# The bias of the last layer norm of block 2 moves from ScalarE to GpSimd, and ScalarE squares the tile before the bias is added

## The reference, cut to what matters

```python
def _layer_norm(x, g, b):
    mu = jnp.mean(xf, -1, keepdims=True)
    var = jnp.mean(jnp.square(xf - mu), -1, keepdims=True)
    return ((xf - mu) * lax.rsqrt(var + LN_EPS) * g + b).astype(x.dtype)

h = _layer_norm(ALPHA * h + ff + ple, ln2_g[i], ln2_b[i])     # end of block 2

def _rmsnorm(x, w):
    y = xf * lax.rsqrt(jnp.mean(xf * xf, axis=-1, keepdims=True) + NORM_EPS)
    return (y * w).astype(x.dtype)

h = _rmsnorm(x, norm_w[l])                                    # start of block 3
proj = h @ w_in[l] + b_in[l]
```

## Time and profile before

| | |
|---|---|
| median of three runs | 3994.99 us |
| the profiled execution's own time | 3996.76 us |
| its span, first to last instruction | 3995.0 us |
| mean granted TensorE clock | 0.983 of full |
| PE busy | 3836.1 us, 96% |
| DVE busy | 1816.0 us, 45% |
| ACT busy | 796.1 us, 20% |
| POOL busy | 592.4 us, 15% |

### The profile page before, as it was taken

The page is one execution under the profiler, slowest core; times in us unless marked ns, Lnnn a source line. Parts: engine busy times, 40 slices in busy tenths (PEclk is TensorE's granted clock), DMA queues, the critical chain, the costliest instruction groups (busy, mean ns, idle before and its releaser), DMA issues.

```text
span 3995.0 us, 32255 instructions
## 1 busy us (share of the span) xinstructions
PE 3836.1 (96%) x12831; PEld 1955.9 (49%) x12831; DVE 1816.0 (45%) x2613; ACT 796.1 (20%) x977; POOL 592.4 (15%) x630
## 2 busy tenths in 40 slices
PE   8999999999899899989999999999899999899998
PEld 4555444544346776454444444444356554544554
DVE  8576434435655542255633232324645553424432
ACT  2112111111452211351310000000323320221121
POOL 0343210122112220132122222222000000000000
PEclk9998999999999999999999999999999999999999
DMA  5332121111011110200111111111101001012101
GB/s 143 82 72 81 42 64 33 42 42 42 22 42 43 27 43 16 74 22 17 58 42 42 42 42 42 42 43 44 38 19 38 24 9 48 14 32 84 32 11 53
DMA packets 291233, 175.01 MB, mean 44 GB/s; under 512 B 24103, under 2 KB 281998, under 8 KB 290830
## 3 DMA queue, kind: packets, MB, share of 16 engines
q1 hardware_dynamic: 264736, 132.24, 12.2%
q0 software_dynamic: 9424, 22.30, 2.1%
q10 hardware_dynamic: 16926, 18.43, 1.4%
HBM read 159.72 MB, written 13.21 MB: 43 GB/s over the span
## 4 chain that ended last, share of the span: by engine, by line
PE 87%; DVE 8%; ACT 2%; issue 1%; POOL 1%; DMA 0%; ACTq 0%; DVEq 0%; POOLq 0%
PE products L359 39%; PE products L161 10%; PE products L3336 8%; PE products L3349 3%; PE products L2523 3%; PE products L1735 3%; DVE work L1446 2%; PE others L3415 2%; PE products L2532 1%; PE products L179 1%; PE others L2398 1%; PE others L2411 1%; PE others L1877 1%; ACT work L214 1%; PE others L2719 1%
## 5 line engine op out<-in xcount | busy, mean ns | idle before, releaser
L359 PE MATMUL products<-gate,s_small 128*128 128x512 f32 x752 | 334.6, 592 | 0.0
L3336 PE MATMUL products<-normed,weights 128*128 128x512 f32 (+2 forms) x704 | 314.8, 596 | 3.7 <-DVE normed L845 3.7
L161 PE MATMUL products<-normed,weights 128*128 128x512 f32 x704 | 309.1, 599 | 8.8 <-DVE s_small L4080 4.0
L359 PE MATMUL products<-work,s_small 128*128 128x512 f32 x640 | 289.1, 596 | 3.3 <-DVE residual L427 2.2
L377 POOL TENSOR_TENSOR s_small<-weights 128x512 f32<-128x512 f32 x66 | 86.6, 1312 | 1268.1 <-PE products L359 1128.1
L359 PE MATMUL products<-normed,s_small 128*128 128x512 f32 x512 | 232.0, 596 | 3.2 <-DVE row L415 2.2
L359 PEld LDWEIGHTS products<-gate,s_small 128*128 128x128 f32 x752 | 142.9, 190 | 179.8 <-issue 179.8
L161 PEld LDWEIGHTS products<-normed,weights 128*128 128x128 f32 x704 | 133.9, 192 | 176.4 <-issue 164.9
L214 ACT ACTIVATE s_small<-products 128x512 f32<-128x512 f32 (+1 forms) x72 | 44.6, 621 | 847.9 <-PE products L359 825.7
L359 PE MATMUL products<-normed,weights 128*128 128x512 f32 x448 | 203.9, 598 | 3.0 <-ACT normed L214 3.0
L3336 PEld LDWEIGHTS products<-normed,weights 128*128 128x128 f32 (+2 forms) x704 | 123.7, 182 | 158.4 <-issue 156.6
(11 more groups left out here) (516 smaller groups left out, 5937.8 us busy)
## 6 DMA issues: line engine op xcount, KB each, us to landing
weights<-in_w_in_dram SPq DMA_DIRECT2D x83, 512.0 KB, 3.9
weights<-in_w_up_dram SPq DMA_DIRECT2D x32, 512.0 KB, 4.8
weights<-in_w_down_dram SPq DMA_DIRECT2D x32, 512.0 KB, 4.6
weights<-in_sgu_w_in_dram SPq DMA_DIRECT2D x24, 512.0 KB, 5.1
weights<-in_s_w_in_dram SPq DMA_DIRECT2D x16, 512.0 KB, 4.7
weights<-in_w_out_dram SPq DMA_DIRECT2D x24, 256.0 KB, 2.8
branch_scratch<-work POOLq DMA_DIRECT2D x8, 512.0 KB, 2.9
work<-branch_scratch POOLq DMA_DIRECT2D x64, 64.0 KB, 2.6
```

The source lines that it names most:

```text
L161: last = pe.matmul(out[0:cols, half * BANK:(half + 1) * BANK], slot(c, b, kt, cols)[:, k, :], acts[n][:, half * BANK:(half + 1) * BANK], s ...
L359: last = pe.matmul(bank, w[:, k * P:(k + 1) * P], moving[k], start=(k == 0 and n in (1, 3, 5)), stop=(k == KT // 2 - 1), skip_group_check= ...
L3336: last = pe.matmul(out[0:cols, half * BANK:(half + 1) * BANK], slot(c, f.b, kt, cols)[:, kk, :], acts[kk][:, half * BANK:(half + 1) * BANK ...
```

## The change

ScalarE no longer adds the bias in this one norm. It squares the scaled tile with the bias inside the activation (Square(x + bias)) straight from `scaled`. GpSimd adds the bias to the tile in place, once ScalarE has read it (`square_ready`), and counts `normed` up. The multiplies of the rms norm on VectorE wait until all eight tiles have their bias.

```diff
 def rms_phase(c, src, dst, gain, sums=None, squared=None, source=None):
     def vector(dve):
         taken(c, dve, g)
+        if source is not None:
+            dve.wait_ge(c.normed, source + KT)
 def ln_phase(...):
         for k in range(KT):
             act.wait_ge(c.scaled, scaled + k + 1)
-            act.activation(dst[:, k, :], dst[:, k, :], ACT.Identity, bias=bias[:, k:k + 1]).then_inc(c.normed, 1)
-            phase.between(act, k)
-            if then_squares is not None and k:
-                act.wait_ge(c.normed, normed + k)
-                square_for_sum(c, act, dst[:, k - 1, :], k - 1, then_squares[1])
-        if then_squares is not None:
-            act.wait_ge(c.normed, normed + KT)
-            square_for_sum(c, act, dst[:, KT - 1, :], KT - 1, then_squares[1])
+            if then_squares is None:
+                act.activation(dst[:, k, :], dst[:, k, :], ACT.Identity, bias=bias[:, k:k + 1]).then_inc(c.normed, 1)
+                phase.between(act, k)
+                continue
+            if k >= 2:
+                act.wait_ge(c.square_used, then_squares[1] + k - 1)
+            act.activation(c.tmp[:, k % 2, :], dst[:, k, :], ACT.Square, bias=bias[:, k:k + 1]).then_inc(c.square_ready, 1)
+
+    def gpsimd(pool):
+        if then_squares is None:
+            return
+        for k in range(KT):
+            pool.wait_ge(c.square_ready, then_squares[0] + k + 1)
+            pool.tensor_scalar(dst[:, k, :], dst[:, k, :], bias[:, k:k + 1], 0.0, ALU.add, ALU.add).then_inc(c.normed, 1)
-    phase = Phase(tensor=tensor, scalar=scalar, vector=vector)
+    phase = Phase(tensor=tensor, scalar=scalar, vector=vector, gpsimd=gpsimd)
-        norm = then(rms_phase(c, c.X, c.B, c.vec["norm_w_3"], squared=norm.squared))
+        norm = then(rms_phase(c, c.X, c.B, c.vec["norm_w_3"], squared=norm.squared, source=norm.normed))
```

More of the change, by code:

```diff
@@ L819, in mean_of_total, with rms_phase @@
     last.then_inc(c.group_done, 1)
-def rms_phase(c, src, dst, gain, sums=None, squared=None):
+def rms_phase(c, src, dst, gain, sums=None, squared=None, source=None):
     g = c.plan.groups
```

## The result

The changed kernel takes 4004.73 us in the median (3999.78 to 4008.75, 12 runs) against 3994.89 us (3992.09 to 3998.72, 12 runs) for the kernel before: a ratio of 1.0022 with a 95% interval of 1.0013 to 1.003. It is slower by 9.8 us. The forecast was 3992.3 us, the range ended at 3997.5, and slower had been given 4 chances in 100.

The account below looks back on a forecast made before the run. TensorE, busy 96% of the span, was taken as the bound. Earlier squares less VectorE's turns with GpSimd end the sum of squares 2.7 us sooner: 3994.99 - 2.7 = 3992.3 us, range 3988.5 to 3997.5.

Parts of the forecast that it names:

- What bounds the kernel now: TensorE, 96% busy; what the end of the sum of squares gains or loses reaches the kernel's end almost whole.
- What the change removes: Eight ScalarE Identities of 1.15 us go; TensorE's first sum-of-squares pass comes at 2855.8 instead of 2859.2 us.
- the new Square: ScalarE's Square with a bias operand was taken at 1.15 us, like Identity with bias.
- The adds on GpSimd: Eight bias adds at 1.12 us each, 9.0 us over 17 us; the rms multiplies' new wait costs nothing.
- What the adds do to VectorE: Adds 3 to 5 take turns with VectorE's last four multiplies, 0.85 us each, 2.55 us together.
- The Trainium skill's lock: A two-SBUF-input VectorE instruction and a GpSimd instruction reading SBUF exclude each other; the first issued keeps the port to its end.
- No turns taken: One-input adds don't stop VectorE's multiplies; the sum of squares ends at 2872.5 us, gain 3.9 us, 3991.1 us; chance 0.15.
- GpSimd comes first: GpSimd's adds win against VectorE; multiplies 1 to 4 each lose 0.93 us; no change, 3995.0 us; chance 0.12.
- The clock doesn't come back: TensorE's clock stays at half for all 32 sum-of-squares passes, ending 7.2 us later: 4002.2 us; chance 0.05.
- The add costs 2.5 us: Turns on VectorE take 3.5 us a tile from multiply 2; sum of squares some 5 us later, 4000 us; chance 0.03.
- The sum: The end of the sum of squares moves from 2876.36 to 2873.67 us, -2.7 us, giving a median of 3992.3 us.

Follow-up runs that it names:

- e1: The changed kernel with GpSimd multiplying by the bias and by 1.0 instead of adding the bias and 0.0: 3995.58 us, ratio 1.0001.
- e2: The changed kernel with GpSimd adding the bias and multiplying by 1.0 instead of adding 0.0, same result: 3993.84 us, ratio 0.9996.
- e6: The changed kernel, add-add kept, but each multiply of the rms norm waits only for its own tile's add: 3998.27 us, ratio 1.0008.
- e5: The changed kernel with add and multiply by 1.0 on GpSimd, adds 3 to 7 only after VectorE's last multiply by the root: 3992.48 us, ratio 0.9996.
- e8: The changed kernel without GpSimd: ScalarE adds the bias where it has time, each rms multiply waits for its own tile: 3999.56 us, ratio 1.0007.
- e4: The changed kernel with the eight adds on VectorE, behind its last multiply by the root, instead of on GpSimd: 3992.09 us, ratio 0.9989.
- e10: The kernel of e4 run once more, with a second profile: 3989.14 us, ratio 0.999.
- e7: The changed kernel with add-add on GpSimd for tiles 0 to 3 only, VectorE adding the bias to tiles 4 to 7: 3998.75 us, ratio 1.0008.
- e12: The kernel of e7 run once more: 3997.2 us, ratio 1.0009.
- e3: A program of its own timing GpSimd tensor_scalar forms alone and beside VectorE multiplies: add-add 3.70 us, three other pairs 1.12 us at 128x1024.

## Why the prediction was wrong, step by step

**What bounds the kernel now: right.** The place was the only one that moved by the edit, and TensorE's waits there arrive at the end.

**What the change removes, and the new Square: right.** TensorE begins after 6.58 us (forecast 6.6), and each biased Square takes 1.15 us.

**The adds on GpSimd: this step failed.** "The arithmetic differs (add and add for multiply and multiply) ... I take 1.12." The term was 3.70 us. The difference was named and then waved through, and the bound from above, 2.5 us from a two-input operation, was no bound: it came from another operation, as did the row. From 8 x 1.12 = 9.0 us "spread over 17 us" became 32.1 us, and with it the next sentence fell, that the new wait "ends before the row is ready, and costs nothing": it costs 11.9 us. e1 and e2 put the price right and change nothing else, and the wait is gone; e6 leaves the price and takes away the wait for the last add, and most of the loss is gone.

**What the adds do to VectorE: right for the fast pair.** e2 has the four multiplies at 7.46 us (4.87 + 2.55 = 7.42 forecast), the last of them ends at +21.23 (forecast 2870.43 - 2849.23 = +21.20), the sum at +24.45 (+24.44), the projections 28.16 behind block 2 (28.2). The Trainium skill's lock ("SBUF — State Buffer", "Who interferes with whom") so holds for a one-input tensor_scalar too, which no row of before could show. That it is kept to the end of the instruction does not hold for add-add: in the changed kernel the multiply issued at 2857.23, 0.05 us behind an add that ran for 3.69 us, ended after 2.13 us, so it was kept out for about 1 us (it takes 1.28 us alone), and two of the last four multiplies took 1.27 us while an add was running.

**The rivals.** "No turns taken" is refuted by e2. "GpSimd comes first" did not occur with the fast pair: multiplies 1 to 4 took 1.28 us in e1 and e2. With add-add, multiply 3 came behind the second add and took 2.13 us. "The clock doesn't come back" was at the wrong place: it came back in the sum of squares, and fell later, in the 15.6 us that the adds made. "The add costs 2.5 us" had the right suspicion, 0.03 of chance, and the wrong mechanism: it spaced VectorE's multiplies 3.5 us apart from multiply 2 on, where only two of them took 0.9 us longer, and it did not see the wait of the rms multiplies.

**The sum.** With the price right, the -2.7 us are there at the start of the projections, and -1.0 us at the 64th pass: 1.7 us went to a fall of the clock there (29.4 us for the 64 passes in e1 and e2). The prediction had taken them at 27.7 us for granted. The medians of e1 and e2, +0.2 and -1.6 us, decide nothing here: both intervals hold -2.7 us, -1.0 us and no change.

What stays open: why the clock falls behind +25 to +29 in e1, e2, e5 to e8 and not in before, e4 and e10, and behind +654 in e2, e6, e7, e8 and e12 and not in the others. e4 and e5 have the same times on TensorE up to the projections and differ in the fall, so neither the idle gaps of the sum nor the start of the projections explain it; e1 and e2 have the same times up to +633 and differ behind it.

## What to carry to other kernels

A duration is taken over from a row only where the operations are the same, not just the instruction, the shape and the operands: on GpSimd, add-add at 128x1024 took 3.3 times as long as add-multiply with 1.0, which computes the same. Where the nearest row is of another operation, the range must hold a multiple of it; and where a wait for the last of several is new, it is priced for the dear end as well as the cheap one. Work that is only due later (here the bias, due at the rms multiplies) can go into the idle time of the engine that will need it: VectorE's 5.4 us of adds cost nothing here, and with them the medians lie 3.3 and 5.6 us under the kernel before (e4 and e10; the first interval ends just below no change, the second at it). Fast adds on GpSimd behind the last multiply (e5) gave the same +27.1 us in the place.

## What the runs showed of the hardware that was not expected

- GpSimd's tensor_scalar, float32, 128x1024: 1.12 us for multiply-multiply, add-multiply and multiply-add; 2.85 us for one operation alone; 3.70 us for add-add, add-subtract, subtract-subtract and subtract-multiply. For add-add 1.145 us at 256, 1.996 at 512 and 3.702 at 1024 elements; for multiply-multiply 0.69 and 1.12 us.
- An add-add of 3.7 us kept a two-input multiply of VectorE out for only about 1 us of it (e3: 0.8 us lost by each of two multiplies).
- In five of the twelve traces (e2, e6, e7, e12, e8) TensorE's clock fell to 1.2 GHz of 2.4 for 10.2 us behind +653, worth 5 us of its work; in e1, with the same times of TensorE to 0.03 us up to +633, it did not. What calls the fall is open.
